# Splitting the seams between the sublayers of a two-block transformer by token tile, on one core

## The chip, the cores and the metric

The kernel runs on one core of one Trainium2 chip. The metric is the device time of one execution, in microseconds (us); lower is better. A core has five engines that run beside each other and meet at semaphores: TensorE (PE; its weight loads are listed as PEld), VectorE (DVE), ScalarE (ACT), GpSimd (POOL) and SyncE (SP, which only issues transfers here).

## The reference, cut to what matters

Two blocks of two layers each work on 256 tokens of 1024 features, all in float32. The change touches the first block only:

```python
def first_block(x, mem, ...):
    for l in range(2):
        x = layer_norm(ALPHA * x + 0.5 * swiglu_ffn(x, ffn_w_in[l, 0], ffn_w_out[l, 0]), ln_g[l, 0], ln_b[l, 0])
        x = layer_norm(ALPHA * x + mixer_sublayer(x, w_mix_in[l], ...), ln_g[l, 1], ln_b[l, 1])
        x = layer_norm(ALPHA * x + memory_cross_attention(x, mem, ...), ln_g[l, 2], ln_b[l, 2])
        x = layer_norm(ALPHA * x + 0.5 * swiglu_ffn(x, ffn_w_in[l, 1], ffn_w_out[l, 1]), ln_g[l, 3], ln_b[l, 3])
    return x
```

`layer_norm` takes the mean and variance of each token's row and then applies a gain and a bias per feature. The second block (adaptive modulation, two kinds of attention, two feed-forward layers, on x and on a context) starts from this x. Its modulation vectors, `silu(c) @ mod_w + mod_b`, don't depend on x, so their products are free to be done at any time before they are used.

## The kernel before, in words

**Number format.** Each float32 matrix product is three products of rounded parts: every operand is a high part (`whi`, `xh`, `uh`) and a low part (`wlo`, `xl`, `ul`), and `hi*hi + hi*lo + lo*hi` is summed in PSUM. Weights come from HBM in blocks of 256 rows x 512 columns (512 KB). `stage` (L455) handles a block: SP loads it into one of 5 `raw` buffers, ACT writes `whi` (L163), DVE writes `wlo = raw - whi` (L122) into one of 4 slots. A slot is free again when the matmuls of the block four back are done (`s_use`). `next_block` (L489) is called as a block's matmuls are emitted and stages the block three further on (`AHEAD`), so each engine's own instruction stream holds the staging of a later block at that place.

**Products.** `gemm` (L512) has the activations stationary and two PSUM banks, one per tile of 128 tokens; each block of weights does both tiles, 12 matmuls of 512 columns, before the next block starts. `gemm_t` (L541) has the weights stationary and leaves the result transposed: 24 matmuls of 256 columns a block. `tiled_gemm` (L569) makes the modulation products straight from the `raw` buffer ("plain" blocks, no split); four blocks form a group, with a small product after it.

**A seam.** Every sublayer of the first block ends in a `gemm` with two columns of 512 features: the feed-forward (`ffn1`, L1179, output `ffn_w_out`, three blocks a column in its last third), the mixer (L1219, `w_mix_out`, four blocks a column), the cross attention (`cross`, L1763, `xa_wo`, two blocks a column). `residual` (L1002) adds each column to `y` and takes its statistics (L144). Then comes `layer_norm` (L718), in this order on the engines: for both tiles the aggregate and the power -1/2 (DVE, POOL), `y = (y - mean) * rstd` (L129); then 16 transposes of `y` on PE (L174) into four banks, each of two features blocks and both tiles; then, bank by bank, DVE applies gain and bias in PSUM (L129, `lncol`), ACT copies to `xh`, DVE writes `xl`. The next sublayer's first product needs `xh`, `xl` and its own split weights. `between_layers` (L781) fills the waits of a seam: it emits the first half of the norm, some work ("before", 3.5 us by the planner's own costs), the second half, and some work ("after"). The work is two modulation blocks each time, except at the mixer's seam, where it is the four blocks of the product for the memory's keys (`keys`, two before, one and the rest after). A `rows` job then writes `x`, the normed rows with gain and bias, on DVE. There are seven such seams: two after the mixer, two after the cross attention, three after a feed-forward. The last feed-forward of the block (in `rows`, L2556) has another norm and is not touched.

**Order of the work.** There is no scheduler on the chip: the whole program is a Python generator that runs once per engine and writes that engine's instructions in order, and each engine runs its list in order. `run`, `fill` and `tick` (L339 to L364) give side jobs a turn after each block. `weave` (L410) merges the x chain and the context chain of the second block and puts modulation blocks in where neither can go on; `modulated` (L925) makes a chain issue modulation blocks itself until enough are there.

**Bias copies.** `rpb_scratch` (L1151) runs beside the first layer's second feed-forward. It copies a 57 KB row of biases 64 times to HBM, in 8 transfers of 448 KB issued by POOL (L302, L119). On POOL's queue the loads of the next norm's `lg` and `lb` (L680), which wait for DVE, stand between the first copy and the other seven.

Of the kernel before, what the change touches and what calls it, by code (L numbers as in the profile page):

```python
# [22 lines left out]
KB = 2  # L23
# [186 lines left out]
def new_core(nc, A, parts, order, live=None, e=None):  # L210
# [21 lines left out]
    for u, b in enumerate(order or ()):  # L232
        co.nth.append(-1 if b[5] else len(co.block_of))
        if not b[5]:
            co.block_of.append(u)
    co.jobs = []
# [252 lines left out]
def next_block(co, w, k0, nk, c0, n, plain=False):  # L489
# [10 lines left out]
    return u, v  # L500

# [10 lines left out]
def gemm(co, xt, xdep, w, c0, n, evac, k0=0, kn=None):  # L512
# [5 lines left out]
    for k in range(0, kn, KB):  # L518
# [19 lines left out]
        yield nk * n * 0.00272  # L538

# [163 lines left out]
def last_norm(co, y, ydep, stats, eps):  # L703

    norm, cen, out = [], [], []
    for t in range(2):
        tok, n = norm_rows(co, y, t, ydep[t], stats[t], eps)
        norm.append(n)
        co.dv.wait_ge(tok, ydep[t], co.lnpar)
# [8 lines left out]
def layer_norm(co, y, ydep, stats, eps, at, nxt):  # L718


    tok, norm, n = [], [], []
    for t in range(2):
        a, b = norm_rows(co, y, t, ydep[t], stats[t], eps)
        tok.append(a)
        norm.append(b)
    for t in range(2):
        co.dv.wait_ge(tok[t], norm[t], ydep[t])
        n.append(co.dv.tensor_scalar(y[:, t, :], y[:, t, :], co.mv[:, t, 0:1], co.rs[:, t, 1:2], ALU.subtract, ALU.mult).then_inc(co.s_dv))
    co.rsfree, co.xready = n[1], None
    yield  # L730
    into = co.xt
    into.dep, at8 = [], 32 * at[0] + 8 * at[1]
    banks, got = [], []
    for k0 in range(0, 8, 2):
        b = next_bank(co, hold=True)
        co.pe.wait_ge(b.drained, n[0], n[1])
        for k in (0, 1):
            for t in range(2):
                r = y[:, t, (k0 + k) * P:(k0 + k + 1) * P]
                m = co.pe.transpose(b.ap[:, k * 256 + t * P:k * 256 + (t + 1) * P], r, ident(co, r)).then_inc(co.s_pe, k == 1 and t == 1)  # L740
        banks.append((b, m))
    turned_ = m

    def part(i):
        b, a = got[i]
        v = co.xt.lo[:, 2 * i:2 * i + 2, :].rearrange("p k n -> p (k n)")
        co.dv.wait_ge(a, into.free)
        v = co.dv.tensor_tensor(v, b.ap, into.hi[:, 2 * i:2 * i + 2, :].rearrange("p k n -> p (k n)").bitcast(F32), ALU.subtract).then_inc(co.s_dv)
        b.drained, b.held = (a, v), False
        into.dep.append((a, v))  # L750

    for i, (b, m) in enumerate(banks):
        co.dv.wait_ge(m, co.lncdep)
        for k in (0, 1):
            o, c = b.ap[:, 256 * k:256 * k + 256], at8 + 2 * i + k
            v = co.dv.tensor_scalar(o, o, co.lncol[:, c:c + 1], co.lncol[:, 64 + c:65 + c], ALU.mult, ALU.add).then_inc(co.s_dv)
        co.ac.wait_ge(v, into.free)
        got.append((b, co.ac.activation(into.hi[:, 2 * i:2 * i + 2, :].rearrange("p k n -> p (k n)"), b.ap, ACT.Copy).then_inc(co.s_ac)))
        if i > 0:
            part(i - 1)  # L760
    part(3)

    def rows():
        out = []
        yield
        for t in range(2):
            x = co.x[:, t, :]
            co.dv.wait_ge(co.lnpar, co.xfree, n[t])
            a = co.dv.tensor_tensor(x, y[:, t, :], co.lg[:, :], ALU.mult).then_inc(co.s_dv)
            yield  # L770
            co.dv.wait_ge(a)
            out.append(co.dv.tensor_tensor(x, x, co.lb[:, :], ALU.add).then_inc(co.s_dv))
            if t == 0:
                yield
# [256 lines left out]
def setup(co):  # L1031
# [21 lines left out]
    for i in range(4):  # L1053
        cs = slice(256 * i, 256 * i + 256)
        co.xready.append(co.sp.dma_start(co.x[:, :, cs], x[:, :, cs]).then_inc(co.s_x[i], by=16))
        if i < AHEAD:
            stage(co, i)
# [1705 lines left out]
```

## Time and profile before

| | us |
|---|---|
| median of 3 runs | 2725.87 (2724.16 to 2730.23) |
| the profiled execution, its own time | 2722.6 |
| its span, first to last instruction | 2720.8 |
| PE busy | 2572.1 (95%) |
| DVE busy | 1703.8 (63%) |
| ACT busy | 1238.1 (46%) |
| POOL busy | 176.2 (6%) |

The mean granted TensorE clock is 0.978 of full. In a row of the profile, L122 is a line of the kernel (often that of a helper), `out<-in` names the buffers without their numbers, and the bracket at the end gives the idle time of the engine just before and what ended it.

### The profile page before, as it was taken

To read this page: it belongs to the slowest core of one execution; us is meant where nothing else is said; L and a number is where in the kernel's file an instruction comes from. 1 tells how busy PE (TensorE), PEld (TensorE's weight loads), DVE (VectorE), ACT (ScalarE), POOL (GpSimd) and SP (SyncE) were. 2 spreads that over 40 slices of the span, in tenths; PEclk is the share of its full clock that TensorE was granted. 3 is DMA by queue.
4 is the path that set the end of the run, shared out by engine and by line. 5 is a ranking of instruction groups with operands and counts; after the bars stand their busy time and mean duration, and the time that the engine had idled before them with its cause. 6 is when DMAs were issued, how large, how long until landed. Compare 5 with 4: busy or idle time off the path is not lost. (4 is left out here: it accounts for less than half of the span.)

```text
span 2720.8 us, 48647 instructions
## 1 busy us (share of the span) xinstructions
PE 2572.1 (95%) x16525; PEld 2212.8 (81%) x16525; DVE 1703.8 (63%) x2500; ACT 1238.1 (46%) x1737; POOL 176.2 (6%) x215
## 2 busy tenths in 40 slices
PE   8999999999999999999899998999999999878999
PEld 8988877888888888878788876878888896656898
DVE  4556776765465465767775667775655566645555
ACT  4435445434344435454454564555443443533443
POOL 1000000010011000000010201200000001100000
PEclk9999999999999999999999999999999999988999
DMA  7655456576566564456566535453556657335664
GB/s 236 210 177 169 147 164 191 173 244 218 185 220 215 188 226 137 137 158 202 169 215 186 160 101 166 150 157 99 164 172 208 211 179 200 119 99 179 200 185 136
DMA packets 276177, 479.66 MB, mean 176 GB/s; under 512 B 17616, under 2 KB 87320, under 8 KB 275872
## 3 DMA queue, kind: packets, MB, share of 16 engines
q1 hardware_dynamic: 265632, 445.24, 51.5%
q0 software_dynamic: 10304, 31.31, 3.7%
q8 instruction: 138, 2.26, 0.3%
q14 instruction: 103, 0.84, 0.1%
HBM read 475.33 MB, written 6.92 MB: 177 GB/s over the span
## 5 line engine op out<-in xcount | busy, mean ns | idle before, releaser
L122 DVE TENSOR_TENSOR wlo<-raw,whi 128x1024 fp32r<-128x1024 f32 (+3 forms) x786 | 911.8, 1172 | 722.5 <-ACT whi L163 597.8
L163 ACT ACTIVATE whi<-raw 128x1024 fp32r<-128x1024 f32 (+3 forms) x786 | 786.5, 1016 | 609.5 <-PE bank L171 454.2
L171 PE MATMUL bank<-xh,whi 128*128 128x256 f32 x2208 | 629.0, 285 | 17.8 <-ACT whi L163 10.6
L171 PE MATMUL bank<-xl,whi 128*128 128x256 f32 x2208 | 620.9, 281 | 0.0
L171 PE MATMUL bank<-xh,wlo 128*128 128x256 f32 x2208 | 620.7, 281 | 0.0
L171 PEld LDWEIGHTS bank<-xh,whi 128*128 128x128 f32 x2208 | 418.0, 189 | 35.8 <-issue 16.3
L171 PEld LDWEIGHTS bank<-xl,whi 128*128 128x128 f32 x2208 | 417.9, 189 | 1.1 <-issue 0.5
L171 PEld LDWEIGHTS bank<-xh,wlo 128*128 128x128 f32 x2208 | 417.8, 189 | 0.0
L171 PE MATMUL bank<-whi,xh 128*128 128x512 f32 (+2 forms) x632 | 257.0, 407 | 11.1 <-DVE wlo L122 3.3
L171 PE MATMUL bank<-wlo,xh 128*128 128x512 f32 (+2 forms) x632 | 249.3, 394 | 0.0
L171 PE MATMUL bank<-whi,xl 128*128 128x512 f32 (+2 forms) x632 | 249.2, 394 | 0.0
L171 PE MATMUL bank<-whi,uh 128*128 128x512 f32 x528 | 211.0, 400 | 3.6 <-DVE sa L122 1.9
L171 PE MATMUL bank<-wlo,uh 128*128 128x512 f32 x528 | 208.5, 395 | 0.0
L171 PE MATMUL bank<-whi,ul 128*128 128x512 f32 x528 | 208.5, 395 | 0.0
L171 PEld LDWEIGHTS bank<-whi,xh 128*128 128x128 f32 x632 | 121.3, 192 | 50.0 <-issue 19.8
L171 PEld LDWEIGHTS bank<-whi,xl 128*128 128x128 f32 x632 | 121.3, 192 | 27.5
L171 PEld LDWEIGHTS bank<-wlo,xh 128*128 128x128 f32 x632 | 121.5, 192 | 24.9 <-issue 0.5
L122 POOL TENSOR_TENSOR cst<-cst 128x8 f32<-128x8 f32 (+4 forms) x50 | 77.4, 1560 | 745.9 <-DVE cst L129 745.9
L171 PEld LDWEIGHTS bank<-whi,uh 128*128 128x128 f32 x528 | 99.0, 187 | 31.8 <-issue 6.8
L171 PEld LDWEIGHTS bank<-whi,ul 128*128 128x128 f32 x528 | 99.0, 187 | 24.1
L171 PEld LDWEIGHTS bank<-wlo,uh 128*128 128x128 f32 x528 | 99.1, 188 | 22.4
L171 PE MATMUL bank<-x2h,whi 128*128 128x256 f32 x352 | 101.0, 287 | 4.5 <-issue 3.1
(431 smaller groups left out, 3886.2 us busy)
## 6 DMA issues: line engine op xcount, KB each, us to landing
raw<-in_ffn_w_in SPq DMA_DIRECT2D x280, 512.0 KB, 4.5
raw<-in_ffn_w_out SPq DMA_DIRECT2D x154, 512.0 KB, 4.5
raw<-in_w_mix_in SPq DMA_DIRECT2D x112, 512.0 KB, 3.6
raw<-in_mod_w SPq DMA_DIRECT2D x96, 512.0 KB, 5.2
raw<-in_od_w_in SPq DMA_DIRECT2D x40, 512.0 KB, 4.5
raw<-in_ffn_w_in SPq DMA_DIRECT2D x56, 256.0 KB, 2.8
raw<-in_w_branch SPq DMA_DIRECT2D x24, 512.0 KB, 3.6
raw<-in_ev_w_in SPq DMA_DIRECT2D x24, 512.0 KB, 3.8
```

The costliest lines, as they stand in the source:

```text
L122: return Made(self.e and self.e.tensor_tensor(out, a, b, op))
L163: return Made(self.e and self.e.activation(out, a, f, **k))
L171: return Made(self.e and self.e.matmul(out, lhs, rhs, **k))
```

## The change: what it does

It has four parts.

**By tile.** The second column of the last product runs tile by tile (`gemm_by_tile`): all weight blocks for tile 0, then all for tile 1. The residual, the statistics and the whole first half of the norm of tile 0 are emitted after tile 0's pass, those of tile 1 after tile 1's pass. No block of weights is staged inside, except that a block of the column that has not been staged yet is staged ahead of it, and `stage_part` stages the next split block (and the plain ones ahead of it) between the passes.

**The norm by tile.** `LayerNorm.steps` first transposes tile 0 (two banks of four features blocks); ACT applies gain and bias to it, one `activation(Identity, scale, bias)` per 128x128, and copies it to `xh`. Then comes the filling work, once. Then tile 1 is transposed into three banks (2, 2 and 4 features blocks), DVE applies gain and bias to these, ACT copies, DVE writes all the `xl` parts.

**Order at the seams.** The "after" work is gone: a seam has two modulation blocks in place of four. With `keep` (all seams but the mixer's) the modulation blocks stage nothing; the second and third split blocks of the next product are staged between the parts of tile 1. At the mixer's seam two of the keys' blocks stand between the halves, and the other two behind.

**Pacing.** Each of the eight bias copies waits on POOL for the PE work emitted up to there.

The diff, cut:

```diff
-def next_block(co, w, k0, nk, c0, n, plain=False):
+def next_block(co, w, k0, nk, c0, n, plain=False, ahead=True):
...
-        stage(co, u + AHEAD)
+        if ahead and not (co.keep and u + 1 < co.staged):
+            stage_to(co, u + AHEAD)
     return u, v
+
+def stage_part(co):
+    while co.order is not None and co.staged < len(co.order):
+        co.staged += 1
+        stage(co, co.staged - 1)
+        if not co.order[co.staged - 1][5]:
+            return
...
+def gemm_by_tile(co, xt, xdep, w, c0, evac, k0, kn):
+    hi, lo = xt
+    banks = [next_bank(co, hold=True) for _ in range(2)]
+    blocks = [(k, min(KB, kn - k)) + next_block(co, w, k0 + k, min(KB, kn - k), c0, 512, ahead=False) for k in range(0, kn, KB)]
+    if co.order is not None:
+        stage_to(co, blocks[-1][2])
+    for t in range(2):
...
+        for k, nk, u, v in blocks:
+            if t == 0:
+                co.pe.wait_ge((co.s_hi, v + 1))
+                co.pe.wait_ge((co.s_lo, v + 1))
+                co.pe.wait_ge(parts_of(xdep, k, nk))
+            for i in range(nk):
...
+                if t == 1:
+                    m = m.then_inc(co.s_use, i == nk - 1)
+                else:
+                    m = m.then_inc(co.s_pe, k + i == kn - 1)
+        evac(banks, m, (t,))
+        banks[t].held = False
+        if t == 0:
+            stage_part(co)
...
+class LayerNorm:
+    def tile(self, t):
+        tok, norm = norm_rows(co, y, t, self.got[t], self.got[2 + t], self.eps)
+        co.dv.wait_ge(tok, norm, self.got[t])
+        self.n[t] = co.dv.tensor_scalar(y[:, t, :], y[:, t, :], co.mv[:, t, 0:1], co.rs[:, t, 1:2], ALU.subtract, ALU.mult).then_inc(co.s_dv)
...
+    def steps(self):
+        for k0 in (0, 4):
+            b, m = self.turn(0, k0, 4)
+            co.ac.wait_ge(m, co.lncdep)
+            for k in range(4):
+                o, (g, s) = b.ap[:, k * P:(k + 1) * P], self.column(k0 + k)
+                a = co.ac.activation(o, o, ACT.Identity, scale=g, bias=s).then_inc(co.s_ac)
+            first.append((b, self.high(b, 0, k0, 4, a)))
+        yield
+        second = [(k0, nk) + self.turn(1, k0, nk) for k0, nk in ((0, 2), (2, 2), (4, 4))]
+        half = [self.low(first[0][0], 0, 0, 4, first[0][1])]
+        for k0, nk, b, m in second:
+            co.dv.wait_ge(m, co.lncdep)
+            for k in range(nk):
+                o, (g, s) = b.ap[:, k * P:(k + 1) * P], self.column(k0 + k)
+                v = co.dv.tensor_scalar(o, o, g, s, ALU.mult, ALU.add).then_inc(co.s_dv)
+            a = self.high(b, 1, k0, nk, v)
+            if k0 == 0:
+                half.append(self.low(first[1][0], 0, 4, 4, first[1][1]))
+            elif co.keep:
+                stage_part(co)
+            co.xt.dep += [(half[k0 // 4], self.low(b, 1, k0, nk, a))] * (nk // 2)
...
-def between_layers(co, norm, work, before, after):
-    next(norm)
-    fill(co, work, before)
-    end(norm)
-    fill(co, work, after)
-    spawn(co, co.after, 2)
+def between_layers(co, norm, work, us, keep):
+    steps = norm.steps()
+    next(steps)
+    co.keep = keep
+    fill(co, work, us)
+    end(steps)
+    co.keep = False
...
                 for t in tiles:
                     got[2 + t] = norm_stats(co, y, t, c0 // 512, got[t])
+                    if norm is not None and c0:
+                        norm.tile(t)
...
     for c in range(0, 64, 8):
         part = bass.AP(tensor=src.tensor, offset=src.offset, ap=[[0, 8], [1, 7 * 16 * P]])
+        co.po.wait_ge(pe_mark(co))
...
-        between_layers(co, norm, co.mods, 3.5, 3)
+        between_layers(co, norm, co.mods, 3.5, True)
...
-        between_layers(co, norm, keys, 3.5, 2)
+        between_layers(co, norm, keys, 5.5, False)
```

In the mixer the memory's transposes (`kv.turn()`) still stand between the first column and the second.

## Rows read from the trace of the kernel before

**Rows 1.** The page's part 1, busy time and share of the span.
```profile
PE 2572.1 (95%) x16525; PEld 2212.8 (81%) x16525; DVE 1703.8 (63%) x2500; ACT 1238.1 (46%) x1737; POOL 176.2 (6%) x215
```

**Rows 2.** Timeline of PE, first feed-forward seam: start us, duration us, engine, line.
```profile
203.21 1.07 PE L171 MATMUL bank<-raw,ch 128*32 128x256 f32 x16
208.69 3.42 PE L174 MATMUL bank<-cst,y 128*128 128x128 f32 x16 [4.40 <-DVE y L129]
212.04 1.07 PE L171 MATMUL bank<-raw,ch 128*32 128x256 f32 x16
...
217.75 0.36 PE L171 MATMUL bank<-xh,whi 128*128 128x256 f32 x1 [1.59 <-ACT whi L163]
```

**Rows 3.** Timeline of DVE, the same seam.
```profile
203.32 1.28 DVE L122 TENSOR_TENSOR y<-y,bank 128x512 f32<-128x512 f32 x2 [5.92 <-PE bank L171]
...
206.86 1.77 DVE L129 TENSOR_SCALAR y<-y,mv,rs 128x1024 f32<-128x1024 f32 x2 [0.45 <-POOL rs L122]
208.55 1.22 DVE L122 TENSOR_TENSOR wlo<-raw,whi 128x1024 fp32r<-128x1024 f32 x1
```

**Rows 4.** Busy time of each engine by stretch, then granted clock, DMA share, GB/s.
```profile
208.60:212.00 3.40, 3.31 (x16) 3.19 (x16) 3.32 (x7) 0.82 (x2) 0.00 (x0) 0.54 0.00 0
621.00:626.00 5.00, 4.31 (x25) 4.34 (x26) 3.04 (x3) 1.62 (x2) 0.00 (x0) 0.63 0.76 243
1159.30:1162.60 3.30, 0.05 (x1) 0.00 (x0) 3.20 (x9) 0.00 (x0) 0.00 (x0) 1.00 0.54 161
1162.60:1166.00 3.40, 3.36 (x13) 2.82 (x14) 1.55 (x4) 3.39 (x5) 0.54 (x1) 0.71 0.68 206
```

**Rows 5.** Timeline of PE, first cross attention's seam.
```profile
558.15 1.07 PE L171 MATMUL bank<-raw,ch 128*32 128x256 f32 x16
559.15 1.05 PE L171 MATMUL bank<-cst,modr 128*128 128x2 f32 x8
...
572.92 0.36 PE L171 MATMUL bank<-xh,whi 128*128 128x256 f32 x1 [1.68 <-issue]
```

**Rows 6.** Lines of ACT, shapes apart: busy us, mean ns, idle before.
```profile
L163 ACT ACTIVATE whi<-raw 128x1024 fp32r<-128x1024 f32 x706 | 736.8, 1056 | 579.6 <-PE bank L171 424.3 <-DMA raw<-in_ffn_w_in 82.7 <-DMA raw<-in_ffn_w_out 46.0
L163 ACT ACT_TABLE_LOAD x34 | 43.6, 1283 | 4.7 <-DMA ctx<-in_ctx 3.4 <-PEq L2752 0.7
...
L163 ACT ACTIVATE pc<-bank,cst 128x256 f32<-128x256 f32 x24 | 11.4, 474 | 17.9 <-DVE cst L128 17.9
L163 ACT ACTIVATE po<-bank 128x256 f32<-128x256 f32 x32 | 11.2, 376 | 19.3 <-DVE po L132 18.8 <-PE bank L171 0.4
```

**Rows 7.** Lines of DVE, shapes apart.
```profile
L129 DVE TENSOR_SCALAR bank<-bank,lncol 128x256 f32<-128x256 f32 x56 | 27.3, 544 | 0.3
```

**Rows 8.** Timeline of PE, the first mixer's seam and the second's last row.
```profile
485.43 0.48 PE L171 MATMUL bank<-whi,xh 128*128 128x512 f32 x1
...
502.55 1.94 PE L174 MATMUL bank<-cst,y 128*128 128x128 f32 x16
512.56 0.39 PE L171 MATMUL bank<-xh,whi 128*128 128x256 f32 x1 [0.99 <-ACT xk L163]
...
1301.74 0.39 PE L171 MATMUL bank<-xh,whi 128*128 128x256 f32 x1 [2.59 <-DVE xk L128]
```

**Rows 9.** Timeline of DVE, ahead of the first mixer's last column.
```profile
489.70 2.35 DVE L122 TENSOR_TENSOR wlo<-raw,whi 128x1024 fp32r<-128x1024 f32 x2
```

**Rows 10.** DMA issues from 596 to 626 us: KB each, us to landing.
```profile
rpb_rows<-rpb_one POOLq DMA_DIRECT2D x7, 448.0 KB, 12.4
...
raw<-in_ffn_w_in SPq DMA_DIRECT2D x1, 512.0 KB, 20.2
```

**Rows 11.** Timeline of PE, in the first layer's second feed-forward.
```profile
621.69 0.55 PE L171 MATMUL bank<-xh,whi 128*128 128x256 f32 x1 [6.49 <-ACT whi L163]
```

**Rows 12.** Timeline of PE, the last modulation blocks: the first and the last row.
```profile
2500.47 1.50 PE L171 MATMUL bank<-raw,cst 128*32 128x256 f32 x24
...
2517.32 1.08 PE L171 MATMUL bank<-raw,cst 128*32 128x256 f32 x8
```

More of the change, by code:

```diff
@@ L235, in new_core @@
             co.block_of.append(u)
+    co.staged, co.keep = 0, False
     co.jobs = []
@@ L715, in last_norm @@
     co.rsfree, co.xready = out[1], tuple(out)
[L718 to L734, printed above, removed]
-        b = next_bank(co, hold=True)
-        co.pe.wait_ge(b.drained, n[0], n[1])
-        for k in (0, 1):
-            for t in range(2):
[L739 to L773, printed above, removed]
-                yield
-        co.xready = tuple(out)
-        if nxt:
-            load_ln(co, nxt[0], nxt[1], out[1])
-    co.after = rows()
@@ L997, in ffn, with residual, evac @@
         for c in range(2):
-            yield from gemm(co, (uh, ul), udep, w_out, c * 512, 512, out(g, c * 512), 8 * g, min(8, 22 - 8 * g))
+            k0, kn = 8 * g, min(8, 22 - 8 * g)
+            if by_tile and (g, c) == (2, 1):
+                yield from gemm_by_tile(co, (uh, ul), udep, w_out, c * 512, out(g, c * 512), k0, kn)
+            else:
+                yield from gemm(co, (uh, ul), udep, w_out, c * 512, 512, out(g, c * 512), k0, kn)
         ufree = pe_mark(co)
-def residual(co, y, scale, got, fe, last=0):
+def residual(co, y, scale, got, fe, last=0, norm=None):
     def make(g, c0):
-        def evac(banks, tok):
-            for t in range(2):
+        def evac(banks, tok, tiles=(0, 1)):
+            for t in tiles:
                 o, p = y[:, t, c0:c0 + 512], banks[t].ap
@@ L1017, in evac @@
             if g == last:
-                for t in range(2):
+                for t in tiles:
                     got[2 + t] = norm_stats(co, y, t, c0 // 512, got[t])
-        return evac
-    return make
-def normed(co, y, got, eps, at, nxt):
-    return layer_norm(co, y, (got[0], got[1]), (got[2], got[3]), eps, at, nxt)
+                    if norm is not None and c0:
+                        norm.tile(t)
+        return evac
+    return make
 def setup(co):
@@ L1192, in ffn1 @@
     co.base = base
-    return normed(co, co.y, got, 4e-5, (l, 3 * i), () if i == 0 else (1, 0))
+    return norm
 def pair(co, dst, banks, tok, a, n, *after):
@@ L1727, in mixer @@
     mdep += to_t(co, lambda t, k: mg[:, t, (4 + k) * P:(5 + k) * P], 4, (co.xt.hi[:, 4:8, :], co.xt.lo[:, 4:8, :]), (mgd[1, 0], mgd[1, 1]), co.xt.free)
-    res = residual(co, y, ALPHA, got, counts(co))
-    for c in range(2):
-        run(co, gemm(co, xt, mdep, A["w_mix_out"][l], c * 512, 512, res(0, c * 512)))
-        if c == 0:
-            kv.turn()
+    norm = LayerNorm(co, y, got, 1e-5, (l, 1), (l, 2))
+    res = residual(co, y, ALPHA, got, counts(co), 0, norm)
+    run(co, gemm(co, xt, mdep, A["w_mix_out"][l], 0, 512, res(0, 0)))
+    kv.turn()
+    run(co, gemm_by_tile(co, xt, mdep, A["w_mix_out"][l], 512, res(0, 512), 0, 8))
     co.xt.free = pe_mark(co)
-    return normed(co, y, got, 1e-5, (l, 1), (l, 2)), kv
+    return norm, kv
 class Memory:
@@ L1842, in cross @@
     got = {}
-    res = residual(co, y, ALPHA, got, fe)
-    for c in range(2):
-        run(co, gemm(co, (oh, ol), odep, A["xa_wo"][l], c * 512, 512, res(0, c * 512)))
+    norm = LayerNorm(co, y, got, 1e-5, (l, 2), (l, 3))
+    res = residual(co, y, ALPHA, got, fe, 0, norm)
+    run(co, gemm(co, (oh, ol), odep, A["xa_wo"][l], 0, 512, res(0, 0)))
+    run(co, gemm_by_tile(co, (oh, ol), odep, A["xa_wo"][l], 512, res(0, 512), 0, 4))
     co.base = start
-    return normed(co, y, got, 1e-5, (l, 2), (l, 3))
+    return norm
 class Stream:
```

77 lines of the change are left out of this document (68 added, 9 removed).

## The prediction

> **What bounds the kernel.** I read the busy shares first: PE is busy 95% of the span [rows 1], so the change can only give back PE's idle time (149 us in all), or time in which PE runs at less than full clock. Then I read PE's timeline at a seam. After the last product PE does two modulation blocks, stands for 4.40 us until DVE has normed `y`, does 16 transposes, two more modulation blocks and the first block of the next product, and stands again for 1.59 us for a split weight [rows 2]. DVE's timeline of the same seam shows why: residual and statistics of both tiles, then both norms, then the second tile's `y` done at 208.63 [rows 3]. The clock view adds a second price: during the 16 transposes the granted clock was 0.54, that is near the lower level of 1.2 GHz, after the 4.40 us of idle PE; they took 3.42 us there, against 1.94 at the mixer's seam, where the keys' blocks leave no idle time before them [rows 2, 4, 8]. So a seam after a feed-forward or the cross attention (five of the seven) has some 5 to 6 us to give plus 1.5 of slow clock; a mixer's seam has nothing at the norm, only waits of 0.99 and 2.59 us for the bank of `xk` [rows 8]. Last, one gap inside a feed-forward: 6.49 us [rows 11].
>
> I count a seam from the end of its last product, T, to the start of the third block of the next product, since everything late is caught up there. A block is 24 matmuls, from 213.11 to 216.16 in these rows, of which 0.2 is the last one's tail: 2.85 us [rows 2]. Before, a seam is 217.75 + 2.85 - 203.21 = 17.4 us at the first feed-forward seam [rows 2] and 572.92 + 2.85 - 558.15 = 17.6 at the first cross seam [rows 5].
>
> **Step 1, the norm of tile 0 moves under tile 1's pass.** For both tiles, residual to normed `y` takes 208.63 - 203.32 = 5.3 us on DVE. For one tile it is that less half of 1.28, 1.28 (the statistics, as long as the residual) and 1.77, plus some 0.25 since each step now waits for the whole of the one before: 3.4 us. Tile 1's pass is half of three blocks, 4.2 us, in the feed-forward. DVE does tile 0's chain (3.4), then the first split weight's `wlo` (1.2, now queued ahead of tile 1's residual): it is free at T + 0.3, and tile 1's `y` is done at T + 3.7. PE meanwhile transposes tile 0 (1.0 at full clock) and does two modulation blocks (1.07), then waits from T + 2.1 to T + 3.7. I keep the full clock there: the matmul after a wait of 1.59 or 2.59 us takes 0.36 and 0.39 us, against 0.55 after the one of 6.49 [rows 2, 8, 11].
>
> **Step 2, tile 1 to `xl`.** Each part is a chain across engines: DVE gain and bias (256 columns take 0.544 [rows 7], 128 are taken as 0.41, two of them 0.7), ACT copy (0.38 as `po<-bank` [rows 6]), DVE `xl`. The first product can start at T + 6.2. Before its second block, ACT has to do the copy, then `whi` (1.06 [rows 6]), DVE `wlo` (1.2), `xl` (0.4): 3.6 us from the start of the first, whose matmuls take 2.85. Before the third, four gain steps (1.4), copy (0.6), `whi`, `wlo`, `xl` (0.65) come one after the other: 4.8 us more. So the third block starts at T + 6.2 + 3.6 + 4.8 = T + 14.6, with new PE waits of about 0.8 and 1.9 us: what is late next is ACT and DVE splitting weights inside the norm's chain. Gain at a feed-forward seam: 17.4 - 14.6 = 2.8, three times 8.4.
>
> At a cross seam tile 1's pass is two blocks, 2.8 us, so tile 0's chain and `wlo` end at T + 1.8, tile 1's `y` at T + 5.3 and the third block starts at T + 16.0. Gain 17.6 - 16.0 = 1.6, twice 3.2.
>
> **Step 3, gain and bias of tile 0 on ACT.** Eight `activation`s with two pointer operands. One pointer costs 474 - 376 = 98 ns at 256 columns [rows 6]. For 128 columns with two, the bounds are 0.38 (no less than a 256-column one without pointers) and 0.57 (256 columns with two); with ACT overlapping neighbours by 0.1, I take 0.4 each, nearest the middle: 3.2 us, plus two copies, from T + 0.6 to T + 5.1. In the feed-forward it costs 0.2 us (it is in the 6.2 of step 2), at a cross seam nothing, DVE being later. The Trainium skill (ScalarE: Activation LUTs, Rules for kernel authors) says to put adds and multiplies on VectorE, not ScalarE. By that rule, taken as twice DVE's time (0.8 each), ACT would be free at T + 8.3 and the first product some 2.5 us later at five seams, so the sum would be 12 us worse. Here 256 columns take 544 ns on DVE and 474 with one pointer on ACT [rows 6, 7], so the trace doesn't agree, and the sum goes by the rows.
>
> **Step 4, the mixer's seams.** Three costs and no gain. (a) The last column needs all four split blocks within tile 0's pass. PE starts it at 485.43 [rows 8] and wants the fourth 3 x 1.4 us later, at 489.6; that block's `wlo` sits behind the memory's low parts and starts at 489.70 [rows 9], done at 490.9: 1.3 us. (b) Only the keys' first block is staged early. Their second, third and fourth are now emitted after ACT's eight gains and two copies: ACT is free at T + 5.1, `whi` to 6.1, `wlo` to 7.3. PE has 1.0 of transposes and 2.85 of the first block, to T + 3.9: it stands 3.4 us (bounds 2.5, if the gains take 0.3, to 4). I take 3.2. (c) After such a gap the clock falls: 0.71 in the 3.4 us after a stretch of 3.3 us in which PE did next to nothing [rows 4]; near 30% of 3.4 us is 1.0 (0 to 1.6). The waits for `xk` stay as they are: the same two blocks end ahead of the same copies. Sum 5.5 a seam, twice 11.0.
>
> **Step 5, modulation blocks put off.** Five seams do two fewer: ten. They are inside the 17.4 and 17.6, so their work comes back later: 0.54 each bare (1.07 for two [rows 2]), 5.4, and 2.5 groups' small products at 1.0 [rows 5], 2.5: at most 7.9 us. The second block needs them before its second norms, between some 1650 and 2100 us, where PE is nearly full. Bounds 0 (all in idle time) and 7.9 (none); I take 6, near the latter, since they are issued there as work of a chain with products around it.
>
> **Step 6, the bias copies.** Seven copies issued together landed after 12.4 us each, and one weight load took 20.2 us beside them [rows 10]; PE then stood 6.49 us [rows 11], and the next block ran at a granted clock of 0.63 over 5 us [rows 4]: 24 matmuls in 4.4 us instead of 2.85. Paced, a copy comes every three blocks, 8.5 us, beside three weight loads, so its 448 KB add less than a third to their 1,536 KB. Gap and slow block go: 6.5 + 1.6 = 8.1 (bounds 5 and 9). POOL's queue waits hold only later copies and the `lg`, `lb` loads, all done long before the next norm: nothing.
>
> **Sum.** -8.4 - 3.2 + 11.0 + 6 - 8.1 = -2.7 us against the profiled execution's 2722.6, so 2719.9. The median of the runs is 3.3 above that execution; against the median it is 2725.87 - 2.7 = 2723.2 us. I keep to the median. A measurement tells about 0.2%, 5.45 us, from no change.
>
> **Rivals.**
> A, the sum above: 2723.2. Chance 0.42.
>
> B, the keys' second block is not late: ACT's gains are quicker than I think or its split is done in the shade of something. Then (b) and (c) of step 4 go, 2 x 4.2 = 8.4: 2714.8. For it: the other costs of step 4 are small, and the five seams' gain doesn't depend on it. Against: the order of emission puts `whi` behind ten ACT instructions. It also stands for the case that the deferred blocks are hidden (6 us, 2717). Chance 0.36.
>
> C, slower: the deferred modulation blocks run bare. In the last such stretch 12 blocks took from 2500.47 to 2518.40, 1.5 us each [rows 12], since each needs a 512 KB load of its own and hides only 0.54 us. Ten at 1.5, plus the small products, are 17.5 in place of 6: 2734.7. It decides from 14.2 us on, 1.2 us a block, if the context chain in the second block has to wait for them with nothing beside it. For it: the planner counts 1.8 us of cover for each; against: the x chain is there to be woven in. Chance 0.13.
>
> D, the pacing does nothing: PE's marks are already passed when POOL reaches the copies, because POOL waited for DVE ahead of them, and they go out together once more. Then the 8.1 stay: 2731.3. Against: the marks are taken a few blocks apart, later than that wait. Chance 0.09.
>
> One more from the Trainium skill, as a check on step 3: a gain function outside the active table set would need a table load, 1283 ns [rows 6] in ACT's chain, up to 14 times. ScalarE: Activation LUTs, Table sets, says that cheap functions such as identity are in every set, so none would come; no row of before shows Identity.
>
> **Chances.** Faster by over 0.2% (below 2720.4): B whole, 0.36, and 0.05 of A: 0.41. Within: 0.33 of A and 0.05 of D: 0.38. Slower: C, 0.04 of A and 0.04 of D: 0.21. The range reaches below B by 3.8 us, for the bounds of steps 5 and 6 (2711), and up to near C, 2733, leaving out most of C and the far tail of B, 2 in 10.
>
> **What would show it.** Right: PE's wait before `y`'s second transposes 1.6 to 2 us and no row at clock 0.54 at a feed-forward seam; two waits of about 0.8 and 1.9 us ahead of the second and third block; 3 us of idle PE after the keys' first block and 1.3 ahead of the mixer's fourth; ten fewer `raw,ch` blocks ahead of 1360 us; the 6.49 us gap gone, weight loads beside the copies under 8 us. Wrong: no wait at the keys, a gap of 4 us left at the seams, more table loads than 34, or modulation blocks with `mod_w` waits of over 1 us before 2100.

## The result, and the profile after

| | before | after |
|---|---|---|
| median of 5 runs, us | 2725.87 (2724.16 to 2730.23) | 2735.41 (2731.85 to 2738.16) |
| span of the profiled execution, us | 2720.8 | 2731.9 |
| mean granted clock | 0.978 | 0.976 |

The change makes the kernel slower by a third of a per cent: ratio 1.0032, 95% interval 1.0018 to 1.0047. The forecast was 2723.2, range 2711 to 2733. One run of the experiment four_mods_back took 3135.4 us at a granted clock of 0.749; no ratio below counts it.

Busy time and share of the span, part 1 of the page, against [rows 1]:

```profile
PE 2581.6 (94%) x16525; PEld 2222.4 (81%) x16525; DVE 1699.6 (62%) x2507; ACT 1256.9 (46%) x1798; POOL 173.9 (6%) x215
```

PE has the same 16,525 instructions and is busy 9.5 us longer. Its idle time (span less busy time) grew by only 1.6 us, from 148.7 to 150.3. So this page alone says that the loss is not one new wait.

**Where the 11.1 us of the span came from.** I laid PE's instructions of the two traces side by side and took, for those that both have, the start in the one less the start in the other. This lag is negative where a kernel is ahead of the one before; its steps tell what each stretch gained or lost. For the changed kernel and eight of the nine experiments below (times are those of the kernel before, us; one profiled execution of each kernel, while the ratios further down are from all runs):

```
at    the change  four_mods  put_off  bank_held  paced  first_seam  keys_early  mixer_as  last_four
 225     -2.1       -2.2      +1.0     -0.5      -0.7     -1.2        -2.3       -2.7      -0.9
 400     +4.3       -2.5      +7.4     +5.8      -0.5     -0.9        -2.3       -2.6      -0.9
 483     +4.3       -2.5      +7.4     +5.7      -0.5     -0.9        -2.3       -2.6      -0.9
 557     +9.4       +3.4      +6.0     +7.3      -0.7     +3.8        -1.0       +0.2      +3.8
 575     +7.8        0.0      +4.6     +7.3      -0.7     +1.1        -4.4       -3.1      +1.3
 610     +8.4       +1.8      +4.6     +7.5      -0.5     +1.6        -2.6       -1.0      +2.5
 640     +0.3       -6.2      +6.1     +9.2      -8.5     -6.5       -10.6       -9.1      -5.6
 775     -0.1       -7.4      +5.5     +8.3      -9.1     -6.3       -11.9      -10.4      -5.8
 792     -3.9       -8.1      +5.9     +8.4      -8.9     -9.5       -11.2       -9.7      -5.2
 984     -1.7       -7.0      +5.9     +8.5      -9.1     -7.4       -10.8       -9.5      -4.8
1002     -4.5       -9.8      +7.2     +8.3      -9.2    -10.2       -13.5      -11.6      -7.6
1270     -4.6       -9.8      +7.0     +7.9      -8.2     -7.2       -12.5      -12.9      -8.6
1315     -1.5       -6.4      +6.9     +9.3      -8.3     -4.0        -9.9       -7.2      -5.4
1364     -3.1       -7.9      +7.7     +9.4      -8.3     -4.9       -11.3       -8.7      -6.5
1650     -2.4       -7.5      +7.1     +9.3      -8.2     -4.8       -11.7       -8.2      -6.7
1697     -0.4       -7.1      +7.3     +9.3      -8.2     -4.3        -8.1       -7.9      -6.7
1783    +16.1       -7.3     +22.3     +9.3      -8.1    +11.8        -8.2       -8.1      -1.4
2060     +6.5       -7.0     +16.1     +9.4      -8.1     +5.3        -8.6       -7.8      -7.2
2234    +13.4       -7.4     +22.7     +9.3      -8.4    +12.0        -9.0       -8.5      -4.5
2700    +11.1      -10.9     +20.8     +6.4     -11.3    +10.1       -12.3      -11.3      -7.3
```

The three feed-forward seams end near 225, 792 and 1002, the cross seams near 575 and 1364, the mixers' seams lie between 483 and 557 and between 1270 and 1315, the copies between 610 and 640, the inside of the first mixer between 225 and 400, and the second block behind 1364. Read down the first column: feed-forward seams 2.1, 3.8 and 2.8 gained, cross seams 1.6 and 1.5, copies 8.1; mixers' seams 5.1 and 3.1 lost; **6.4 lost inside the first mixer** and **14.2 in the second block**, with 2.2 spread over the rest of the first. Gains 19.9, losses 31.0. The row at 2060 is no measure where blocks are put off: there the second block's two chains stand in another order, and beside +6.5 some instructions of the change have +20.6. At 1697, 1783 and 2234 all agree to 0.5 us. Behind 2234 the lag falls by 2 to 4 us in every kernel of the table, those that change nothing there included; the profiled execution of the kernel before was that much behind the others there, and I have no cause for it.

**A feed-forward seam.** PE's timeline of the first one, against [rows 2]; the columns are those of that group:

```profile
203.75 1.03 PE L174 MATMUL bank<-cst,y 128*128 128x128 f32 x8
204.72 1.07 PE L171 MATMUL bank<-raw,ch 128*32 128x256 f32 x16
207.68 1.09 PE L174 MATMUL bank<-cst,y 128*128 128x128 f32 x8 [1.89 <-DVE y L129]
210.07 0.55 PE L171 MATMUL bank<-xh,whi 128*128 128x256 f32 x1 [1.30 <-DVE xl L122]
```

DVE's timeline there, against [rows 3]:

```profile
202.36 0.81 DVE L129 TENSOR_SCALAR y<-y,mv,rs 128x1024 f32<-128x1024 f32 x1 [0.76 <-POOL rs L122]
203.09 1.22 DVE L122 TENSOR_TENSOR wlo<-raw,whi 128x1024 fp32r<-128x1024 f32 x1
204.23 0.68 DVE L122 TENSOR_TENSOR y<-y,bank 128x512 f32<-128x512 f32 x1
...
206.81 0.81 DVE L129 TENSOR_SCALAR y<-y,mv,rs 128x1024 f32<-128x1024 f32 x1 [0.74 <-POOL rs L122]
```

The first row is tile 0's norm, done 0.6 us before the last product ends at 203.75; the last is tile 1's, done at 207.62, T + 3.9 (forecast T + 3.7). The single wait of 4.40 us has become 1.89 and 1.30, and the first product starts at 210.07, T + 6.3 (forecast 6.2). The clock did what the forecast ruled out. Busy time by stretch and granted clock, against [rows 4]:

```profile
207.60:210.00 2.40, 1.09 (x8) 0.86 (x8) 2.40 (x7) 1.25 (x3) 0.00 (x0) 0.84 1.06 397
210.00:213.00 3.00, 2.93 (x14) 2.96 (x15) 1.55 (x3) 1.33 (x2) 0.00 (x0) 0.50 0.34 131
213.00:216.00 3.00, 3.00 (x16) 3.00 (x16) 1.75 (x6) 1.21 (x2) 0.00 (x0) 0.50 0.56 160
216.00:219.00 3.00, 3.00 (x26) 2.98 (x26) 2.58 (x3) 2.47 (x4) 0.10 (x1) 0.99 0.20 31
```

After idle times of 1.89 and 1.30 us the clock was at 0.50, the level of 1.2 GHz, for 6 us: 16 matmuls in 3 us instead of 26. It cost next to nothing here, since the second and third block would have had to wait for their split weights anyway: no wait stands ahead of either, and the third starts at 218.51, T + 14.8, where T + 14.6 was forecast. With four modulation blocks (first experiment) the clock stayed at 1.00 there, the waits were 1.02, 1.30, 0.76 and 1.51, and the seam gained the same 2 us. The last two of these are the forecast's 0.8 and 1.9 ahead of the second and third block; at half clock they vanish into PE's longer work. So ACT and DVE set this seam, at either clock.

The same waits don't always bring the same clock. keys_split_early has this seam as four_mods_back has it, with waits of 1.03 and 1.30 us, and a granted clock of 0.52 from 210 to 213. And a later fall does cost: first_seam_four and last_four_put_off, at 0.50 and 0.54 from 218.5 to 221.5 behind waits of 1.81 and 1.89 us, stand at -1.2 and -0.9 at 225, where four_mods_back, keys_split_early and mixer_as_before stand at -2.2 to -2.7.

**A mixer's seam.** PE's timeline, first layer's, then the keys' second block of the second layer:

```profile
495.34 0.47 PE L171 MATMUL bank<-whi,xh 128*128 128x512 f32 x1 [1.14 <-issue]
...
509.54 0.51 PE L171 MATMUL bank<-memh,whi 128*128 128x256 f32 x1 [3.24 <-ACT whi L163]
...
1288.12 0.55 PE L171 MATMUL bank<-memh,whi 128*128 128x256 f32 x1 [3.23 <-ACT whi L163]
```

These are (a) of step 4, 1.14 against 1.3, and (b), 3.24 against 3.2; the granted clock over 509 to 513 was 0.57. The waits for `xk`'s bank [rows 8], 0.99 us in the first layer and 2.59 in the second, are gone: the keys came late enough to hide them. So the second seam cost 3.1 and not 5.5.

**The first mixer.** Three waits of PE's timeline. The first and the third had no counterpart in the first mixer before; the second stands where the kernel before had a wait of 2.88 us for `dsl`, and adds about 1 us:

```profile
283.78 1.12 PE L171 MATMUL bank<-sps,cst 128*128 128x512 f32 x2 [1.47 <-DVE zs L122]
...
352.05 0.72 PE L171 MATMUL bank<-ckvt,qlt 128*128 128x128 f32 x4 [3.35 <-ACT lb L163]
...
379.41 0.71 PE L174 MATMUL bank<-cst,dsl 128*128 128x128 f32 x4 [3.27 <-DVE sg L122]
```

**The second block.** Two waits of PE's timeline that grew:

```profile
1748.25 1.97 PE L174 MATMUL bank<-cst,etk 128*128 128x128 f32 x8 [6.18 <-DVE etk L122]
...
1761.09 1.18 PE L174 MATMUL bank<-cst,etk 128*128 128x128 f32 x8 [3.73 <-DVE etk L122]
```

and the stretch around them, by stretch and clock, first of the kernel before:

```profile
1364.00:2720.80 1356.80, 1271.51 (x8074) 1076.60 (x8073) 850.07 (x1331) 631.67 (x934) 104.19 (x89) 0.97 0.53 164
1650.00:1770.00 120.00, 105.82 (x573) 87.82 (x572) 94.45 (x186) 57.52 (x85) 24.23 (x21) 0.96 0.52 162
```

then of the kernel after, whose second block begins 3 us earlier:

```profile
1361.00:2731.90 1370.90, 1282.04 (x8160) 1084.79 (x8160) 852.89 (x1334) 633.98 (x938) 105.29 (x92) 0.97 0.53 166
1650.00:1770.00 120.00, 96.87 (x496) 74.82 (x496) 86.01 (x166) 48.34 (x74) 21.72 (x21) 0.91 0.52 170
```

Over the whole block PE is busy 10.5 us more and idle 3.6 us more. Ten blocks and their small products are 7.9 of that. In the 120 us from 1650 PE issues 77 fewer matmuls, at a clock of 0.91, although 11 modulation blocks stand there in place of 3. By the table the loss comes between 1697 and 1783, where the lag goes from -0.4 to +16.1; 2.7 of it come back by 2234. The same stretch of work, by stretch and clock, first before, then after:

```profile
1697.00:1783.00 86.00, 79.26 (x499) 69.59 (x498) 70.20 (x156) 45.76 (x71) 17.55 (x12) 0.98 0.52 157
```

```profile
1696.60:1799.10 102.50, 88.50 (x573) 75.22 (x572) 77.49 (x179) 50.70 (x76) 22.76 (x18) 0.93 0.56 178
```

It holds 9 modulation blocks in place of 1. The eight more and two small products are 6.3 of the 16.5 us by the forecast's prices, PE's idle time grows by 7.3 (14.0 against 6.7), and the rest is the slower clock.

**The copies.** DMA issues from 596 to 660 us, against [rows 10]:

```profile
raw<-in_ffn_w_in SPq DMA_DIRECT2D x15, 512.0 KB, 7.3
...
rpb_rows<-rpb_one POOLq DMA_DIRECT2D x8, 448.0 KB, 6.2
```

The copies land after 6.2 us and not 12.4, and the gap of [rows 11] is gone: PE has no wait of 0.4 us or more between 600 and 660.

### The profile page after: what moved, and what is told of

It is laid out like the page before. It is cut to its first block and busy times, and to the rows that moved or that the text cites. A ratio compares the mean times of both kernels' runs of the same rounds, so it can differ in the third digit from the quotient of the medians.

```text
span 2731.9 us, 48808 instructions
## 1 busy us (share of the span) xinstructions
PE 2581.6 (94%) x16525; PEld 2222.4 (81%) x16525; DVE 1699.6 (62%) x2507; ACT 1256.9 (46%) x1798; POOL 173.9 (6%) x215
```

## The experiments

Each was timed against the kernel before on the same chip, whose median there was 2722.4 to 2723.0, so ratios are what compares. An expectation that names a span is set beside the profiled span. Names as in the table of lags: four_mods is four_mods_back, and so on.

**Four modulation blocks at each seam again.** The changed kernel with

```diff
-        between_layers(co, norm, co.mods, 3.5, True)
+        between_layers(co, norm, co.mods, 7.0, True)
```

at the three places.

> The changed kernel with four modulation blocks in each seam's one filling (7.0 us by the planner) in place of two, so none is put off. Theory 1 (the ten blocks put off cost 13.6 us in the second block and leave a half-done group, with a PSUM bank, through the first mixer, 7 us): both go, and two more blocks of 0.54 us fall mostly into PE's 1.9 us wait at a seam; span 2731.9 - 13.6 - 7 = 2711 us, the waits at the first mixer's banks (1.5 and 3.3 us) gone, the second block as long as before the change. Rival (the second block and the mixer are longer because of the new order itself, by tile): span 2731 us, both losses stay.

Measured: 2715.72, ratio 0.9969 (0.9958 to 0.9981), span 2709.9. The loss turns into a gain, and the lag shows it in two places: between 225 and 400 it stays at -2.5, and behind 1364 it goes from -7.9 to -10.9 instead of up by 14.2. The other stretches stay near those of the change. At the ends the two profiled executions are 22.0 us apart, and by the ratios of all runs the kernels are some 17 us apart: that is what two modulation blocks fewer at five seams cost, where the forecast had 6. (The fall from -7.9 to -10.9 is the one behind 2234 that all kernels show.)

**The same put off, and nothing else.** The kernel before, with `between_layers(co, norm, co.mods, 3.5, 0)` at the same three places.

> The kernel before, with the filling behind the norm taken out (ten modulation blocks put off), nothing else. Theory 1: the second block 13.6 us longer, the first mixer 7 us longer, each of five seams shorter by the two blocks' 1.07 us: span 2720.8 + 13.6 + 7 - 5.4 = 2736 us. Rival (putting off costs only its own PE time, 0 to 8 us, the rest is the new order): 2716 to 2724 us.

Measured: 2742.04, ratio 1.0071 (1.0059 to 1.0083), span 2741.7. Without any of the change's other parts the first mixer loses 6.4 (lag +1.0 to +7.4) and the second block 13.1 (+7.7 to +20.8). Both losses belong to the putting off. The span is 5.7 us above the 2736 expected, because the seams were not shorter by 1.07 each but the five together 2.1 longer, though two blocks are missing in each. With no work behind the norm the granted clock was 0.51 from 208 to 218, against 0.83 in the kernel before, and 0.50 against 0.84 from 785 to 795 (782 to 792 before) at the next one after a feed-forward: in the old order that filling was worth more than its own time.

**A PSUM bank held.** Two blocks are half of a modulation group, and a group keeps its bank until it is whole. To test that alone, the kernel before, in the first layer's mixer:

```diff
+    spare = next_bank(co, hold=True) if l == 0 else None
...
+    if spare is not None:
+        spare.held = False
```

> The kernel before, with one PSUM bank held and unused from the first mixer's first product until just before its modulation blocks; no instruction is added. Theory 2 (a half-done modulation group takes a bank from the mixer, and the round of banks comes back to ones not yet read): the first mixer gets waits of 1.5 us for zs and 3.3 us for sg, and the span is 4 to 7 us longer, 2725 to 2728 us. Rival (the mixer's loss comes from other timing, such as where side jobs stand): same span as before, 2721 us.

Measured: 2731.35, ratio 1.0032 (1.002 to 1.0044). The lag goes from -0.5 to +5.8 between 225 and 400, as in the change, and the same three waits are there:

```profile
285.27 1.13 PE L171 MATMUL bank<-sps,cst 128*128 128x512 f32 x2 [1.48 <-DVE zs L122]
...
353.45 0.68 PE L171 MATMUL bank<-ckvt,qlt 128*128 128x128 f32 x4 [3.25 <-ACT lb L163]
...
380.83 0.66 PE L174 MATMUL bank<-cst,dsl 128*128 128x128 f32 x4 [3.28 <-DVE sg L122]
```

So one bank fewer, with all modulation work in its old place, is enough for the whole loss in this mixer (6.3 of 6.4 us). The Trainium skill (Perfetto Trace Analysis, Optimizing Tensor Performance) has independent groups of matmuls rotate through the banks so that the emptying of one lies beside the next one's matmuls. By that rule a bank less shows as waits for ACT and DVE, and the trace agrees: 1.48, 3.25 and 3.28 us. The profiled span, 2727.2, lies in the 2725 to 2728 expected; the median went up by 8.4 us. Between 483 and 640 another 3.5 us went, after the bank was free again. Two waits that the kernel before has too are longer there: the one for `xk`'s bank, 2.61 us in place of 0.99, and the one beside the bias copies, 7.95 in place of 6.49. What made them longer stays open.

**Four blocks at the first seam only.** The changed kernel with `7.0 if l == 0 else 3.5` there.

> The changed kernel with four modulation blocks at the first seam only (as before the change) and two at the four other seams. So no modulation group is half done while the first mixer runs, and eight blocks are still put off instead of ten. Theory (two separate losses): the first mixer's 7 us go, the second block's 13.6 us stay or lose a fifth at most. The two blocks cost 1.07 us of their own at the seam but come off the second block. Time of the changed kernel 2735.4 - 7 - 0 to 2.7 = about 2727 us (2724 to 2730). Rival (one loss: all of it is deferral, the first mixer's waits have another cause): only a fifth of it comes back, 2731 to 2734 us, and the waits of 1.47, 3.35 and 3.27 us for zs, lb and sg at 283, 352 and 379 us stay.

Measured: 2728.37, ratio 1.0018 (1.0009 to 1.0027). The waits for zs, lb and sg are gone and the lag stays at -0.9 up to 483. And the second block lost 15.0, with two blocks fewer put off than in the change. In the second layer's mixer the lag rises by 3.0 (-10.2 at 1002 to -7.2 at 1270; by -0.1 in the change), with a wait for `lb` of 4.74 us where the change has 2.78; the cause of that stays open.

It isn't simply a held bank, since every kernel of this study holds one there. The matmuls of the modulation blocks ahead of 1003 us (8 a block) make 41 blocks in the kernel before, 33 in the change and 35 here. None is a multiple of four, so a group stands open all through the second mixer. The kernel before has the three waits there (PE's timeline):

```profile
1067.42 1.13 PE L171 MATMUL bank<-sps,cst 128*128 128x512 f32 x2 [1.49 <-DVE zs L122]
...
1135.31 0.68 PE L171 MATMUL bank<-ckvt,qlt 128*128 128x128 f32 x4 [2.82 <-ACT lb L163]
...
1162.64 0.66 PE L174 MATMUL bank<-cst,dsl 128*128 128x128 f32 x4 [3.29 <-DVE sg L122]
```

From the first matmul on `sps` to the last transpose of `dsl` the kernel before takes 142.3 us in the first mixer and 148.3 in the second; with a bank held in the first, in the change and in bank_held_in_mixer, the first takes 148.7. So the kernel before loses some 6 us in its second mixer in the same way. Closing the group ahead of that mixer was not tried.

**Four blocks put off as one whole group.** The kernel four_mods_back, with no modulation block at the second layer's cross attention (`7.0 if l == 0 else 0`).

> The changed kernel with four modulation blocks at every seam, but none at the second layer's cross attention, the last seam of the first block: four blocks, one whole group, are put off to the second block. With ten put off the second block lost about 14 us, with eight 16; with none it lost nothing. Theory (each block costs its own work and a share of new waits and slow clock, near 1.4 us a block, whatever their number): the second block is 5 to 6 us longer than with all four, and the last seam shorter by 1 at most (its fill only covered a wait): 2715.7 + 4.5 = about 2720 us (2718 to 2722). Rival (a threshold: a few blocks go into idle time, and only many push the context's chain late): the second block is under 3 us longer, 2715 to 2717 us, with no wait of over 4 us for etk near 1745 us.

Measured: 2715.19, ratio 0.9968 (0.9956 to 0.9981), the same as with none put off. The rival's time holds, though not its sign, for a wait for `etk` of 5.34 us stands at 1737.53: four blocks cost 2.2 us of the profiled second block (-6.5 to -7.3, where four_mods_back goes from -7.9 to -10.9), against 3.2 for their own work by the forecast's prices, and nothing that the medians show; eight and ten make it 15.0 and 14.2 us longer than before the change. It isn't one price for each block. What tells these kernels apart is how many modulation blocks stand between 1620 and 1760 us, by the rows of their matmuls there (8 a block): 4 in the kernel before, 4 with four blocks at each seam, 6 here, 10 with eight put off, 12 in the change. The stretch of this kernel, to set beside the two above:

```profile
1650.00:1770.00 120.00, 105.30 (x581) 87.36 (x580) 91.80 (x190) 57.38 (x86) 23.00 (x18) 0.93 0.53 160
```

PE is as busy as before. In the change DVE, too, is less busy in this stretch (86.01 against 94.45 us): no engine there is full, each waits for another. The blocks that the chain issues itself before its second norm stand between steps of the context's attention, whose `etk` PE then awaits. That the crowd in this stretch is the cause is argued from the counts and waits. A wait of over 5 us for `etk` alone doesn't price it: this kernel has one too, loses 5.3 us from 1697 to 1783 and has 3.1 of them back at 2234. I did not try to spread the same ten blocks out, so it stays open which instruction passes the delay on.

**The keys' next split ahead of the norm's gains.** The kernel four_mods_back, in `gemm_by_tile` between the passes:

```diff
         if t == 0:
             stage_part(co)
+            if kn == 8:
+                stage_part(co)
```

> The changed kernel with four modulation blocks at each seam, and the split of one more of the keys' blocks emitted between the two passes of the mixer's last column, so that ACT does it ahead of the ten instructions of tile 0's gain, bias and copy. Measured without this: 2715.7 us. Theory (step 4b and 4c of the prediction): PE's wait of 3.2 us ahead of the keys' second block falls to under 1 us at both mixers' seams, with the slow clock behind it, 3 to 4 us at the first; at the second one part of it comes back as the wait for the bank of xk (2.59 us before the change). Sum 4 to 8 us: 2708 to 2712 us. Rival (ACT is the bound there, whatever the order): the wait moves on to the norm's chain, as ACT's gains come 1.06 us later, and PE waits ahead of the first product instead: 2714 to 2717 us.

Measured: 2710.28, ratio 0.9952 (0.9938 to 0.9965). The wait of 3.2 us ahead of the keys' second block is gone at both seams. The first mixer's seam costs 1.3 (-2.3 to -1.0) in place of 5.9, with 1.05 us for a split in the next product; at the second, the wait for `xk`'s bank is back, as expected (PE's timeline):

```profile
513.05 0.36 PE L171 MATMUL bank<-xh,whi 128*128 128x256 f32 x1 [1.05 <-ACT whi L163]
...
1290.43 0.39 PE L171 MATMUL bank<-xh,whi 128*128 128x256 f32 x1 [2.62 <-ACT xk L163]
```

and that seam costs 2.6 in place of 3.4. So (b) and (c) of step 4 were the order of emission, and one more call mends it. This kernel has the lowest ratio of the study, though its interval overlaps those of the next ones; that the seams are better is read from the waits.

**The mixer's seams as before.** The kernel four_mods_back, with the mixer's last column by `gemm`, and

```diff
+        fill(co, keys, 5.5)
-        between_layers(co, norm, keys, 5.5, False)
+        between_layers(co, norm, keys, 0, False)
```

> The changed kernel with four modulation blocks at each seam, and the mixer's last column done block by block again, with two of the keys' blocks ahead of the first transposes, as in the kernel before; the norm's chain stays split by tile, all of it after the column. Measured without this: 2715.7 us. Theory (the mixer's seams had nothing to gain from passes by tile, and pay 6 and 3.4 us there): these 9.4 us go, less up to 3 us since tile 0's gain on ACT and tile 1's chain now come one after the other behind both tiles' norm: about 2708 us (2704 to 2711). Rival (what costs at this seam is the norm's new chain and not the passes): nothing comes back, 2714 to 2718 us, and a wait of over 2 us stands ahead of the next product.

Measured: 2711.8, ratio 0.9958 (0.9945 to 0.9971). The first mixer's seam costs 2.8 in place of 5.9, but the second costs 5.7 in place of 3.4: with the keys' four blocks in their old place their end meets the copies of `xk`, and the norm's new chain puts those later (PE's timeline):

```profile
511.47 0.58 PE L171 MATMUL bank<-xh,whi 128*128 128x256 f32 x1 [2.04 <-ACT xk L163]
...
1290.47 0.55 PE L171 MATMUL bank<-xh,whi 128*128 128x256 f32 x1 [5.17 <-DVE xk L128]
```

Both sides had a part of it: the wait of over 2 us ahead of the next product is the rival's sign, while the time is nearer the theory's. The median came out 4 us above the 2708 expected and just outside its range, at no difference from keys_split_early that the intervals can tell.

**The pacing alone.** The kernel before with `co.po.wait_ge(pe_mark(co))` ahead of each copy.

> The kernel before with the pacing of the bias copies alone. The theory of step 6 of the prediction: the 6.49 us gap and the slow block behind it go, span 7.4 to 8.1 us shorter, 2713 us. Rival (the gap only moves to another late weight load): under 3 us shorter.

Measured: 2712.6, ratio 0.9966 (0.9954 to 0.9978). The lag falls by 8.0 between 610 and 640, as in the change and as the theory of step 6 has it. The span, 2709.5, is 11.3 us shorter and not 8.1: the rest is the fall behind 2234 that all kernels show. Set beside four_mods_back (0.9969), this says what the seams by tile bring with four blocks kept and the keys not mended: nothing. Their gain at five seams is lost at the two mixers' seams.

**The put-off turned round.** The kernel keys_split_early with eight modulation blocks at the last seam (`7.0 if l == 0 else 14.0`).

> The kernel keys_split_early (2710.3 us) with eight modulation blocks in place of four at the last seam of the first block: the put-off turned round. Theory: the seam's wait is covered by four already, so four more cost there their own 0.54 us each and a small product of 1.0, 3.2 us, if their weights have come; the second block gives back about 1.4 us for each, 5.5: sum -2, about 2708 us (2706 to 2711). Rival (the loads bound it: with nothing to multiply beside them, each block of 512 KB takes about 1.5 us or more, as in the last modulation blocks before): the seam costs 6 to 10 us and the sum is 2711 to 2715 us.

Measured: 2722.7, ratio 0.9995 (0.9986 to 1.0004): 15 us above the theory's time and 8 above the top of the rival's. The second block gave back 4.5 us more than in keys_split_early, close to the 5.5 expected. But the seam lost 14.9 (lag -12.7 at 1345, +2.2 at 1364), where keys_split_early gains 1.4: more than even the rival had. PE's wait, then ACT's and DVE's timelines:

```profile
1351.20 1.01 PE L171 MATMUL bank<-modr,cst 128*2 128x512 f32 x1 [12.00 <-ACT modr L163]
```

```profile
1345.60 1.06 ACT L163 ACTIVATE whi<-raw 128x1024 fp32r<-128x1024 f32 x1 [20.93 <-DMA raw<-in_ffn_w_in]
```

```profile
1346.74 1.22 DVE L122 TENSOR_TENSOR wlo<-raw,whi 128x1024 fp32r<-128x1024 f32 x1 [12.11 <-ACT whi L163]
1347.89 0.68 DVE L132 SCALAR_TENSOR_TENSOR y<-x,bank 128x512 f32<-128x512 f32 x1
```

And the busy time by stretch (the last two numbers are the DMA's busy share and GB/s):

```profile
1331.00:1336.00 5.00, 4.29 (x29) 3.08 (x27) 2.65 (x6) 0.00 (x0) 0.56 (x1) 1.00 0.10 33
1337.00:1346.00 9.00, 2.20 (x35) 1.18 (x35) 0.00 (x0) 0.40 (x1) 0.00 (x0) 0.77 0.89 291
```

Between the passes `stage_part` stages the next split block and the plain ones ahead of it. From 1331 to 1336 the DMA does next to nothing: the `raw` buffers hold modulation blocks, which PE reaches only behind its last product. Then the loads run one after the other at 291 GB/s, and the split block's is behind them on SP's queue. ACT's `whi` is emitted ahead of the gains and waits 20.93 us for that load; the norm's gains and `modr` are queued behind it on ACT, tile 1's residual behind `wlo` on DVE. The rival was right that the loads bound it, but neither had the mechanism: a load that a whole chain of in-order work had been put behind.

## Why the prediction was wrong

**Steps 1 and 2 were right.** 8.4 forecast for the feed-forward seams, 2.1 + 3.8 + 2.8 = 8.7 measured; 3.2 for the cross seams, 1.6 + 1.5 = 3.1 measured. The single seams scatter about the forecast's 2.8 by up to 1 us. The terms that step 2 lists ahead of the second block (copy, `whi`, `wlo`, `xl`) add up to 3.0 and not to the 3.6 that it uses; where the clock stayed full, in four_mods_back, the first, second and third block start at 209.98, 213.79 and 218.42, so 3.8 and 4.6 us apart against 3.6 and 4.8. One assumption was wrong and cost nearly nothing: "I keep the full clock there". It fell to 0.50, which also hid the two waits of 0.8 and 1.9 us at the first seam; at the third, in the change, they are there, 0.58 and 1.70.

**Step 3 was right.** ACT's gain of 128 columns takes 0.37 us from start to start (four in 1.48), against 0.4, and DVE's four take 1.37. Lines of ACT, shapes apart, against [rows 6]:

```profile
L163 ACT ACT_TABLE_LOAD x32 | 41.1, 1283 | 4.8 <-DMA ctx<-in_ctx 3.0 <-PEq L2838 0.7 <-PE bank L171 0.5
...
L163 ACT ACTIVATE bank<-bank,lncol 128x128 f32<-128x128 f32 x56 | 20.7, 433 | 34.2 <-PE bank L174 34.2
```

No table load came with Identity: 32, two fewer than before. The Trainium skill (ScalarE: Activation LUTs, Table sets) says that identity is in every set, and the trace agrees. The forecast had taken the rule of the same page of the Trainium skill (Rules for kernel authors), that adds and multiplies belong on VectorE, as twice DVE's time on ACT; the steps here take 0.37 us on ACT and 0.34 on DVE, about the same.

**Step 4 had its parts right and its sum 2.8 too high**, 11.0 against 5.1 + 3.1 = 8.2. (a) and (b) came to within 0.2 us. "The waits for `xk` stay as they are" was wrong: delaying the keys hid them, 0.99 us in the first layer and 2.59 in the second.

**Step 6 was right:** 8.1 forecast, 8.1 measured.

**Step 5 failed twice.** First, its size: "at most 7.9 us", I wrote, and took 6; the second block lost 14.2. The bound held only the blocks' own work. It left out that ten blocks in a chain can delay that chain's neighbours: between 1697 and 1783, where they crowd, PE's idle time grew by 7.3 us (by 3.6 over the whole block), at a clock of 0.93 there. Rival C's bound, from 14.2 us on, was just met, and its time of 2734.7 lies 0.7 from the result. That nearness is luck: it had 17.5 us for the blocks and no term for the bank, and its mechanism, blocks that run bare at 1.5 us each, would have cost some 7 us for the four of last_four_put_off, where the profile shows 2.2 and the medians nothing. I gave it 0.13. Second, a term is missing altogether: what a half-done group leaves behind. The step counted instructions and not the PSUM bank that they keep; that was 6.4 us in the first mixer, shown alone by bank_held_in_mixer.

With the measured terms: -8.7 - 3.1 + 8.2 + 14.2 - 8.1 + 6.4 + 2.2 (spread) = +11.1 us, the growth of the span. Of the forecast's error of 13.8 us against the profiled execution, 8.2 are step 5's size and 6.4 the bank; step 4's 2.8 too many and the spread 2.2 nearly cancel. The medians are only 9.5 us apart, so the terms hold for these two executions to 2 us or so. What is shown is that both losses come from the putting off, and that a held bank makes the first; how the second is passed on stays open.

## What to carry to other kernels

Before work is put off, ask what it leaves half done: a group that keeps an accumulator bank through the next stage can cost more than the work itself, so count the groups at the start of a stage and move whole ones; here the kernel before, too, enters its second mixer with a group open. A bound for postponed work is not its own time when it is issued inside a dependent chain; here four were nearly free and eight cost 15 us. In engines that run in order, emit the split of the next weights ahead of a chain of small instructions that PE doesn't need at once, but only if its load is surely there.

## What the runs showed of the hardware that was not expected

PE's granted clock fell to 0.50 for 6 us after two idle times of 1.89 and 1.30 us, with its matmuls 0.214 us from start to start in place of 0.119. After 1.02 and 1.30 us at the same place it stayed at 1.00 in four_mods_back, but after 1.03 and 1.30 us it was 0.52 from 210 to 213 in keys_split_early, which has the same instructions there. So these waits alone don't settle the clock. The rows that I had read beforehand show falls behind gaps of 4.40 and 6.49 us [rows 2, 11] and behind a stretch of 3.3 us in which PE did next to nothing [rows 4]; but the trace of the kernel before has shorter ones too, such as 0.50 from 1700 to 1703 behind a wait of 2.17 us, which speaks against the forecast's full clock. The fall cost nothing where PE was ahead of its inputs, in place of waits of 0.8 to 1.5 us, and over 1 us where it came behind them.
